# First attention of a two-layer trunk: stacked query halves and keys held twice for its scores

## What is computed

```python
qkv = h @ w_qkv + b_qkv
q = apply_rope(q, cos[:, None, None], sin[:, None, None]) * (A_HEAD_DIM ** -0.5)
k = apply_rope(k, cos[:, None], sin[:, None])
...
kb, vb = band(kr, km), band(vr, vm)        # meta, previous block, own block
s = jnp.einsum('bnqkgd,bnskd->bnkgqs', qr, kb).astype(jnp.float32)
p = sink_softmax(jnp.where(mask[:, None, None], s, NEG_INF), sink).astype(v.dtype)
o_r = jnp.einsum('bnkgqs,bnskd->bnqkgd', p, vb).reshape(B, n_blk * BLOCK, A_Q_W)
```

## Time and profile before

| | |
|---|---|
| timed runs | 3390.6 us median of 3 (3390.01 to 3392.79) |
| profiled execution, first to last instruction | 3393.5 us |
| busy over the whole span | PE 92%, PE weight loads 73%, DVE 50%, ACT 37%, POOL 54% |
| first attention | 0 to 606 us: start and weights to 75, steps q of 17 tiles to 590, drain to 602 |
| a steady tile | 32.2 us |
| DMA in the steady tiles | 35 GB/s, 11% of the queues' time |

### The profile page before, as it was taken

How to read it: one execution, slowest core, us unless ns; L and a number is a source line. 1 busy time by engine, 2 the same in 40 slices (tenths; PEclk the granted TensorE clock), 3 DMA queues, 4 the chain that set the end, 5 groups by cost and what they waited for, 6 DMA issues and landing times. The chain is left out here.

```text
span 3393.5 us, 56800 instructions
## 1 busy us (share of the span) xinstructions
PE 3126.6 (92%) x19621; PEld 2484.2 (73%) x19621; DVE 1687.2 (50%) x4096; ACT 1242.9 (37%) x2675; POOL 1821.2 (54%) x1447
## 2 busy tenths in 40 slices
PE   6999999899599998799799999999998996999992
PEld 4788887688598897799566666666665885899981
DVE  3555556577344333455365556555661564444333
ACT  2444445222123332444244444444442321332233
POOL 2555555244244443344488888888885222444434
PEclk8999999999799999899699999999998997999996
DMA  3001012644599996455602211221112643999986
GB/s 105 27 28 41 29 40 58 216 149 136 195 328 322 319 317 169 123 160 153 158 10 54 51 26 41 54 51 29 39 60 73 205 149 129 341 320 318 313 240 218
DMA packets 359641, 491.69 MB, mean 145 GB/s; under 512 B 87309, under 2 KB 286753, under 8 KB 357144
## 3 DMA queue, kind: packets, MB, share of 16 engines
q1 hardware_dynamic: 326136, 412.83, 38.7%
q0 software_dynamic: 33312, 76.43, 8.8%
HBM read 362.79 MB, written 135.09 MB: 147 GB/s over the span
## 5 line engine op out<-in xcount | busy, mean ns | idle before, releaser
L2185 POOL TENSOR_TENSOR keep_wg<-keep_wg,ab_pT 128x1024 f32<-128x1024 f32 (+2 forms) x320 | 597.9, 1868 | 90.7 <-ACT ab_pT L2219 48.3
L2219 ACT ACTIVATE ab_pT<-ab_S 128x512 f32<-128x512 f32 (+4 forms) x704 | 349.9, 505 | 511.8 <-PE ab_S L2317 253.7
L2246 DVE TENSOR_REDUCE ab_mx<-ab_W 128x2 f32<-128x800 f32 (+1 forms) x224 | 249.7, 1117 | 207.9 <-PE ab_W L2331 203.2
L1337 POOL DMA_INDIRECT scratch_h<-ex_y,ex_prow x65 | 104.5, 1607 | 437.2 <-ACT ex_yr L1370 258.8
L1509 PE MATMUL ex_G<-ex_xT,keep_wg 128*128 128x160 f32 x2080 | 297.3, 302 | 10.5 <-DMA ex_wu<-in_moe_w_up 10.5
L1509 PEld LDWEIGHTS ex_G<-ex_xT,keep_wg 128*128 128x128 f32 x2080 | 288.1, 192 | 12.1 <-DMA ex_wu<-in_moe_w_up 11.3
L1509 PE MATMUL ex_U<-ex_xT,ex_wu 128*128 128x160 f32 x2080 | 293.1, 299 | 0.0
L1509 PEld LDWEIGHTS ex_U<-ex_xT,ex_wu 128*128 128x128 f32 x2080 | 286.1, 190 | 0.0
L2366 PE MATMUL ab_O<-ab_pT,keep_wg 128*64 128x512 f32 (+4 forms) x1408 | 262.8, 515 | 0.0
L350 POOL TENSOR_TENSOR aa_prob<-aa_prob,aa_rden 128x1024 f32<-128x1024 f32 x68 | 127.4, 1894 | 191.6 <-DVE aa_rden L517 191.6
L1382 DVE TENSOR_TENSOR ex_wd_lo<-ex_wd,ex_wd_hi 128x2048 fp32r<-128x2048 f32 x65 | 149.0, 2292 | 160.2 <-ACT ex_wd_hi L1375 160.2
(11 more groups left out here) (325 smaller groups left out, 7954.1 us busy)
## 6 DMA issues: line engine op xcount, KB each, us to landing
keep_wg<-in_moe_w_gate SPq DMA_DIRECT2D x65, 1024.0 KB, 8.0
ex_wu<-in_moe_w_up SPq DMA_DIRECT2D x65, 1024.0 KB, 10.7
ex_wd<-in_moe_w_down SPq DMA_DIRECT2D x65, 1024.0 KB, 12.4
scratch_h<-pr_h SPq DMA_DIRECT2D x33, 512.0 KB, 5.0
scratch_xn<-pr_xn SPq DMA_DIRECT2D x33, 512.0 KB, 2.7
pr_o<-scratch_oT SPq DMA_DIRECT2D x32, 512.0 KB, 4.7
scratch_qT<-pb_qT SPq DMA_DIRECT2D x17, 768.0 KB, 5.2
scratch_oT<-keep_wg SPq DMA_DIRECT2D x17, 512.0 KB, 2.9
```

Source lines behind the costliest of these rows:

```text
L2185: nc.gpsimd.tensor_tensor(to, to, pT[:, U % RING, :, 0:n], ALU.add).then_inc(added, 1)
L2219: nc.scalar.activation(pT[:, U % RING, h, 0:n], S[:, h, 0:n], ACT.Exp, scale=B_SCALE).then_inc(exped, 1)
L2246: nc.vector.reduce_max(mx[:, :, t, c:c + 1].rearrange("p h a -> p (h a)"), W[:, j % 2, :, 0:n], AX.X).then_inc(emptied, 1)
```

## The change

The scores' contraction is brought to 128 rows. Queries: ACT and DVE write the high and low halves into small buffers (`q_hi`, `q_lo`, 512 columns, one half tile at a time), and SP then copies them by transfers into `q2`, for each group the high part on partitions 0 to 63 and the low part on 64 to 127 (`stack`, four transfers of 64 x 512 each half tile). Keys: POOL writes the rotated keys twice side by side into `k2`, so that a transpose gives the same key on both halves of the partitions; there are two transposes, one for each group, and `k_hi` and `k_lo` hold a band for each of the two groups, in 2 slots instead of 4. One full-height matmul with `k_hi` then gives high x high + low x high, one with `k_lo` gives high x low + low x low: two for each group, four a pair. The previous block of the band is no longer written from PRJ, but copied from the last slot (ACT for `k_hi`, DVE for `k_lo`). The values are kept in a ring of 6 tiles, with a wait. New waits: `raise_q` for the transfers out of the one buffer, the scores at k = 0 and 4 for `stacked`.

```diff
@@ buffers
-        q_hi, q_lo = s.sb("q_hi", [P, 2, DC, P], F32R), s.sb("q_lo", [P, 2, DC, P], F32R)
-        k_hi, k_lo = s.sb("k_hi", [P, 4, BAND], F32R), s.sb("k_lo", [P, 4, BAND], F32R)
-        v = s.sb("v", [P, NT, KVW])
+        q_hi, q_lo = s.sb("q_hi", [P, 4 * P], F32R), s.sb("q_lo", [P, 4 * P], F32R)
+        q2 = s.sb("q2", [P, 2, 2, DC, P], F32R)
+        k_hi, k_lo = s.sb("k_hi", [P, 2, 2, BAND], F32R), s.sb("k_lo", [P, 2, 2, BAND], F32R)
+        k2 = s.sb("k2", [P, 2, 2, HD])
+        v = s.sb("v", [P, VR, KVW])
...
+        flipped_k = PRJ[:, 0:2 * P].rearrange("p (g t) -> p g t", g=2)
@@ SP
+                def stack(n, b):
+                    sp.wait_ge(qk_low, 3 * n + 1 + b)
+                    if n >= 2:
+                        sp.wait_ge(scored, PAIRS * (n - 1))
+                    for g in range(2):
+                        for part, at in ((q_hi, 0), (q_lo, HD)):
+                            sp.dma_start(q2[at:at + HD, g, n % 2, 4 * b:4 * b + 4, :].rearrange("p c t -> p (c t)").bitcast(F32),
+                                         part[HD * g:HD * g + HD, :].bitcast(F32)).then_inc(stacked[b], 16)
...
                 for p in range(0, NT + 1):
...
+                    if live(p + 1):
+                        for b in range(2):
+                            stack(p + 1, b)
@@ POOL
-                    nc.gpsimd.tensor_tensor(qr[:, QW:], qk[:, n % 2, QW:], rot[:, QW:], ALU.add)
+                    twice = [t.rearrange("p (g d) -> p g d", g=2).unsqueeze(2).to_broadcast([P, 2, 2, HD]) for t in (qk[:, n % 2, QW:], rot[:, QW:])]
+                    nc.gpsimd.tensor_tensor(k2[:, :, :, :], twice[0], twice[1], ALU.add)
@@ ACT
-                    if n >= 2:
-                        act.wait_ge(scored, PAIRS * (n - 1))
-                    nc.scalar.copy(q_hi[:, n % 2, 4 * b:4 * b + 4, :].rearrange("p c t -> p (c t)"), PRJ[:, :]).then_inc(qk_high, 1)
+                    if b == 1:
+                        act.wait_ge(stacked[0], 64 * (n + 1))
+                    elif n >= 1:
+                        act.wait_ge(stacked[1], 64 * n)
+                    nc.scalar.copy(q_hi[:, :], PRJ[:, :]).then_inc(qk_high, 1)
...
-                    nc.scalar.copy(k_hi[:, (n + 1) % 4, META:META + P], PRJ[:, 0:P])
-                    nc.scalar.copy(k_hi[:, n % 4, META + P:BAND], PRJ[:, 0:P]).then_inc(qk_high, 1)
+                    if n >= 2:
+                        act.wait_ge(scored, PAIRS * (n - 1))
+                    if n >= 1:
+                        nc.scalar.copy(k_hi[:, n % 2, :, META:META + P], k_hi[:, (n - 1) % 2, :, META + P:BAND].bitcast(F32))
+                    nc.scalar.copy(k_hi[:, n % 2, :, META + P:BAND], flipped_k).then_inc(qk_high, 1)
@@ DVE
+                        if n >= VR:
+                            dve.wait_ge(summed, 10 * (n - VR + 2))
...
-                    nc.vector.tensor_tensor(k_lo[:, (n + 1) % 4, META:META + P], PRJ[:, 0:P], last, ALU.subtract)
-                    nc.vector.tensor_tensor(k_lo[:, n % 4, META + P:BAND], PRJ[:, 0:P], last, ALU.subtract).then_inc(qk_low, 1)
+                    if n >= 1:
+                        nc.vector.tensor_copy(k_lo[:, n % 2, :, META:META + P], k_lo[:, (n - 1) % 2, :, META + P:BAND].bitcast(F32))
+                    nc.vector.tensor_tensor(k_lo[:, n % 2, :, META + P:BAND], flipped_k, last, ALU.subtract).then_inc(qk_low, 1)
@@ PE
-                    nc.tensor.transpose(PRJ[:, 0:P], qr[:, QW:], ident[:, :]).then_inc(flipped_qk, 1)
+                    for g in range(2):
+                        last = nc.tensor.transpose(PRJ[:, P * g:P * g + P], k2[:, g, :, :].rearrange("p a d -> p (a d)"), ident[:, :])
+                    last.then_inc(flipped_qk, 1)
...
+                        if k % 4 == 0:
+                            pe.wait_ge(stacked[k // 4], 64 * (n + 1))
...
-                        for c, (qs, ks) in enumerate(((q_hi, k_hi), (q_hi, k_lo), (q_lo, k_hi))):
-                            for g in range(2):
-                                last = nc.tensor.matmul(S[:, q % 2, g, 0:BAND], qs[HD * g:HD * g + HD, n % 2, k, :], ks[HD * g:HD * g + HD, n % 4, :],
-                                                        start=(c == 0), stop=(c == 2))
+                        for g in range(2):
+                            for c, ks in enumerate((k_hi, k_lo)):
+                                last = nc.tensor.matmul(S[:, q % 2, g, 0:BAND], q2[:, g, n % 2, k, :], ks[:, n % 2, g, :],
+                                                        start=(c == 0), stop=(c == 1))
```

More of the change, by code:

```diff
@@ L316, in _ @@
                 for part in (k_hi, k_lo):
-                    nc.gpsimd.memset(part[:, 0, 0:META + P].bitcast(F32), 0.0)
+                    nc.gpsimd.memset(part[:, 0, :, 0:META + P].bitcast(F32), 0.0)
                 pool.drain().then_inc(zeroed, 1)
@@ L405, in raise_k @@
                         act.wait_ge(zeroed, 1)
[L406 to L409, removed]
-                    nc.scalar.copy(k_hi[:, (n + 1) % 4, META:META + P], PRJ[:, 0:P])
-                    nc.scalar.copy(k_hi[:, n % 4, META + P:BAND], PRJ[:, 0:P]).then_inc(qk_high, 1)
+                        for r in range(2):
+                            nc.scalar.copy(k_hi[:, r, :, 0:META], flipped_k[:, :, 0:META])
+                    if n >= 2:
[3 more added lines that the diff above has]
+                    nc.scalar.copy(k_hi[:, n % 2, :, META + P:BAND], flipped_k).then_inc(qk_high, 1)
                 def job(p, k):
@@ L479, in add @@
                     if g == 2:
-                        last = nc.vector.scalar_tensor_tensor(out=v[:, n, :], in0=PRJ[:, KVW:2 * KVW], scalar=r,
+                        if n >= VR:
+                            dve.wait_ge(summed, 10 * (n - VR + 2))
+                        last = nc.vector.scalar_tensor_tensor(out=v[:, n % VR, :], in0=PRJ[:, KVW:2 * KVW], scalar=r,
                                                               in1=bqkv[:, QW + KVW:QKV], op0=ALU.mult, op1=ALU.add)
@@ L485, in lower_q @@
                     dve.wait_ge(qk_high, 3 * n + 1 + b)
-                    nc.vector.tensor_tensor(q_lo[:, n % 2, 4 * b:4 * b + 4, :].rearrange("p c t -> p (c t)"), PRJ[:, :],
-                                            q_hi[:, n % 2, 4 * b:4 * b + 4, :].rearrange("p c t -> p (c t)").bitcast(F32), ALU.subtract).then_inc(qk_low, 1)
+                    nc.vector.tensor_tensor(q_lo[:, :], PRJ[:, :], q_hi[:, :].bitcast(F32), ALU.subtract).then_inc(qk_low, 1)
                 def lower_k(n):
                     dve.wait_ge(qk_high, 3 * n + 3)
-                    last = k_hi[:, n % 4, META + P:BAND].bitcast(F32)
+                    last = k_hi[:, n % 2, :, META + P:BAND].bitcast(F32)
                     if n == 0:
-                        for r in range(4):
-                            nc.vector.tensor_tensor(k_lo[:, r, 0:META], PRJ[:, 0:META], last[:, 0:META], ALU.subtract)
-                    nc.vector.tensor_tensor(k_lo[:, (n + 1) % 4, META:META + P], PRJ[:, 0:P], last, ALU.subtract)
-                    nc.vector.tensor_tensor(k_lo[:, n % 4, META + P:BAND], PRJ[:, 0:P], last, ALU.subtract).then_inc(qk_low, 1)
+                        for r in range(2):
+                            nc.vector.tensor_tensor(k_lo[:, r, :, 0:META], flipped_k[:, :, 0:META], last[:, :, 0:META], ALU.subtract)
+                    if n >= 1:
+                        nc.vector.tensor_copy(k_lo[:, n % 2, :, META:META + P], k_lo[:, (n - 1) % 2, :, META + P:BAND].bitcast(F32))
+                    nc.vector.tensor_tensor(k_lo[:, n % 2, :, META + P:BAND], flipped_k, last, ALU.subtract).then_inc(qk_low, 1)
                 def job(p, k):
@@ L683, in _ @@
                             for g in range(2):
-                                last = nc.tensor.matmul(O[HD * g:HD * g + HD, P * i:P * i + P], v[:, tile, HD * g:HD * g + HD],
+                                last = nc.tensor.matmul(O[HD * g:HD * g + HD, P * i:P * i + P], v[:, tile % VR, HD * g:HD * g + HD],
                                                         pT[:, u % 3, P * (2 * g + b):P * (2 * g + b) + P],
```

3 lines of the change are left out of this document (added).

## The result

| | before | changed |
|---|---|---|
| timed runs, median | 3391.7 us (4 runs, 3390.0 to 3396.9) | 3421.6 us (4 runs, 3417.6 to 3425.3) |
| profiled execution, first to last instruction | 3393.5 us | 3419.8 us |
| last value product of the first attention starts | 602.2 us | 628.0 us |
| from there to the end | 2791.3 us | 2791.7 us |
| a steady tile | 32.2 us | 34.1 us |

The change costs time: the ratio is 1.0081, with a 95% interval of 1.0066 to 1.0095, that is 22 to 32 us. In the profiled executions the difference is 26.3 us, and all but 0.4 us of it lies in the first attention.

The account below looks back on a forecast made before the run. PE bounds the first attention, busy 99.9 of 100 us. Terms -8.5 - 0.5 + 2.2 + 1.7 + 30.3 + 1.1 + 10 = +36 us give 3427 us, range 3386 to 3440.

Parts of the forecast that it names:

- The held copy: Key split, k 6: DVE's low-key copy waits for POOL's line 367; 2.33 us a tile, 13 times, +30.3 us; chance 0.70.
- Tile 1's keys: Key split for tile 1: line 367 starts later, the copy waits only for POOL's operation ahead, +1.1 us.
- The matmuls and the latency: Score groups: full-height matmuls gain 0.61 us a tile, -8.5; DVE's later maximum costs 0.16 a tile, +2.2.
- The transfers: Stacking queries on SP's queue: ACT's second half waits in tile 15, +1.7 us (0.4 to 3.1); steady tiles covered.
- the rival of late transfers: Steady tiles: transfers come late for ACT, 14 us more, 3403 us without the held copy; chance 0.05.
- The ends: Tiles 0, 15 and 16, which run on chains and not on PE: -0.5 us.
- The clock: PE behind its waits: six falls to 1.2 GHz taken, one losing 1.7 us, +10 us (0 to 22).
- The rival on the other side: At k 7 the longer key chain fits the slack, the matmuls' gain stands nearly alone: 3378 to 3383 us; chance 0.05.
- the latency's term: At k 0, DVE's maximum starts later behind the last of four matmuls: +0.16 us a tile, +2.2 us (0 to 4).

Follow-up runs that it names:

- both copies early: The changed kernel with DVE's copy of the low keys and ACT's copy of the high keys issued at k 2: 3387.4 us, ratio 0.9988.
- the kernel with the matmuls alone: The kernel before, with four full-height score matmuls over unstacked operands for the six row-tiled ones (scores are other numbers): 3387.1 us, ratio 0.9980.
- tile 15 without the transfers' wait: Both copies at k 2, and the last half tile's queries go to `x_hi` and `x_lo`, so ACT needn't wait: 3384.1 us, ratio 0.9982.
- two other kernels: The kernel before plus a DVE copy of 256 SBUF elements: ahead of line 495, 3397.2 us; between lines 495 and 496, 3417.2 us.
- the kernel whose copy wasn't held: The changed kernel, with DVE's copy of the low keys written as 0 x PRJ + k_lo, first input from PSUM: 3394.4 us, ratio 1.0009.
- another kernel: The kernel before, with a DVE copy of 256 SBUF elements added between lines 495 and 496: 3417.2 us, ratio 1.0074.
- all 13 of 3.6 us: The changed kernel, with two more DVE operations, each with a drain, between held copy and subtraction from tile 2 on: 3464.4 us, ratio 1.0209.

## Why the prediction held, and where it didn't

The forecast was 3427 us in a range of 3386 to 3440, and 3421.6 was measured, by the mechanism named. Point by point, on the profiled executions:

- **The held copy**: predicted 2.33 us a tile, 30.3 in all. PE's start lies 2.28 us later than where nothing waits, and pair 7 is 2.37 us longer (6.94 us, and 4.57 with both copies early), 30.8 us for 13 tiles. The order of events was the predicted one to 0.1 us: copy at 0.1 behind line 367's start predicted, 0.18 found; held to POOL's end, as line 1072 in the earlier trace rows.
- **Tile 1's keys**: +1.1 predicted, for a wait on POOL's operation ahead; that copy took 0.99 us and tile 0 is 1.2 us longer.
- **The matmuls and the latency**: -0.61 and +0.16 us a tile, together -0.45. Measured with both copies early: 31.74 less 32.20, -0.46. The spacing of the full-height matmuls was right (0.12 to 0.13 us, taken as 0.125), and so was the second key transpose at 0.11 (pair 6 takes 2.86 us, and 2.75 in the kernel with the matmuls alone). But two parts were off in ways that cancel. The latency hardly costs anything: pairs 0 and 1 together take 4.49 us against 4.48, where the sum has 0.12 more. And pairs 4 and 5 gain nothing (9.57 against 9.56), where the sum has 0.10: at k 4 line 631 starts 0.08 behind the end of DVE's line 511, the low queries, and there are 0.34 to the next matmul as before the change, while at k 2 the 0.34 became 0.23.
- **The transfers**: +1.7 predicted for tile 15, 1.3 measured, with an ACT wait of 1.84 us. In the steady tiles nobody waits for them, as predicted, and the rival of late transfers is out.
- **The ends**: -0.5 predicted for tiles 0, 15 and 16. Tile 0 with both copies early is as long as before (28.76 us), tile 15 without the transfers' wait 0.05 shorter, and from tile 16's first score matmul to the last value product it is 29.85 us against 29.36: +0.5 in place of -0.5. The kernel with the matmuls alone shows 29.83 there, so it comes with the full-height matmuls; why stays open.
- **The clock**: +10 us predicted, nothing found. This is the step that failed. Between one row without a fall behind 1.38 us and one with a fall behind 2.42 I took half of the stretches to fall; at 2.1 us none of them did. Waits of 1.92, 2.11 and 2.15 us in two other kernels did have a fall, so a fall at this length was possible, and nothing in the rows of the kernel before could have told its share. The 13 waits come at the same place of tiles of the same length, and are hardly independent tries; what decides, other than the length, stays open. The sum without that term is +26.3 us, and the profiled executions differ by 26.3. That the two agree to the tenth is luck, since the start of the program alone varies: the first score matmul starts at 75.35 us before and 73.94 after, and in the other kernels, none of which changes the start, between 70.65 and 74.82. From that matmul to the last value product the stage takes 27.3 us more than before, 1.0 above the sum, about what the term of the ends was off by.

The medians differ by 29.9 us and the profiled executions by 26.3; with single executions of the kernel before between 3390.0 and 3396.9, and an interval of the ratio of 22 to 32 us, both are the same finding. The prediction's sum without the clock's term, 3417, is 4.6 us below the measured median, within that scatter. That 3427 lies as near, 5.4 above it, is no merit of the clock's term.

The rival on the other side, a faster kernel from the matmuls' gain alone, didn't occur: it takes two edits that the change doesn't make. Its price was also too good. Forecast was 3378 to 3383 with the last tile's wait in it; the kernel with both copies early, which has that wait, takes 3387.4, and without the wait it is 3384.1. The rival left out the latency's term, and so took the whole 0.61 us a tile where 0.46 is there.

## What to carry to other kernels

Before an SBUF to SBUF copy or cast is put on VectorE in a place that someone waits for, look at what GpSimd runs there and which of the two is issued first: 0.1 to 0.2 us of order was worth 2.0 us a tile, 0.7% of the whole kernel where it hit every steady tile. Such a copy belongs where GpSimd is idle, or on ScalarE, or should take one input from PSUM. And a saving on the bounding engine (0.46 us a tile here) shows only if the chains that feed it keep some slack: the key split had 0.31 us, and with its longer operations the kernel whose copy wasn't held (0.42 us each) came out at 32.19 us a tile, as long as before.

## What the runs showed of the hardware

- A hold works in both directions and is decided by less than 0.1 us: 0.07 behind, DVE's cast took 2.44 us for 0.29 of work; 0.06 ahead, POOL's addition took 2.49 for 2.36 to 2.40.
- The same cast was held, a reduction over the same SBUF elements in the same place wasn't (0.41 us), and neither was an operation with one SBUF and one PSUM input (0.42 us). ACT's cast of the same size from SBUF to SBUF wasn't held either (0.41 us with and without POOL beside it).
- Idle stretches of TensorE of 2.1 us, one in each tile, left the granted clock at 1.00 in all 13 tiles, as did 13 of 1.94 to 1.97 us in another kernel. One of 1.92, one of 2.11 and one of 2.15 us, each in one of the first three tiles, had a stretch at 0.50 in or behind them, as had all 13 of 3.6 us.
- Behind a wait, a 256-column projection's first matmuls stand 0.22 us apart (372.69 to 372.91) in place of 0.12 where nothing waits (with both copies early). So a wait costs more than the profile's idle time shows: 2.11 us idle, PE's start 2.28 us later, and pair 7 longer by 2.37.
- Six row-tiled score matmuls of 272 columns take 0.57 us from the first start to the next group's, four full-height ones 0.61; the next group's first gap is 0.17, 0.34 or 0.22 us behind the former and 0.11, 0.23 or 0.12 behind the latter (transposes at k 0, projections at k 2 and k 7).
